# Stick-breaking q and k of a decoder trunk: products split as 512 + 256 columns, and products of 256 columns only

## What is computed

```python
u = rms_norm(h, mix_pre_g[i])
sb_q, sb_k, sb_v, df_q, df_k, df_v, g_sb, g_df = jnp.split(u @ w_in[i], split_at, axis=-1)

def stick_breaking_attention(q, k, v):          # 8 heads of 64
    z = einsum('bhqd,bhkd->bhqk', q_block, k) * 64 ** -0.5
    log_one_minus = where(strict, log_sigmoid(-z), 0.0)
    later = cumsum(log_one_minus, reverse) - log_one_minus
    w = where(strict, exp(log_sigmoid(z) + later), 0.0)
    return einsum('bhqk,bhkd->bhqd', w, v)
```

## Times and profile before

| | us |
|---|---|
| median of three runs | 1176.17 (1175.84 to 1176.51) |
| the profiled execution | 1175.95 |
| its span on the core | 1174.2 |
| busy: PE (matmul) | 1164.3 (99%) |
| busy: PEld (weight load) | 983.6 (84%) |
| busy: DVE (VectorE) | 849.9 (72%) |
| busy: ACT (ScalarE) | 720.6 (61%) |
| granted TensorE clock, share of full | 0.999 |

### The profile page before, as it was taken

How to read it: one execution, slowest core, us unless ns; L and a number is a source line. 1 busy time by engine, 2 the same in 40 slices (tenths; PEclk the granted TensorE clock), 3 DMA queues, 4 the chain that set the end, 5 groups by cost and what they waited for, 6 DMA issues and landing times.

```text
span 1174.2 us, 17191 instructions
## 1 busy us (share of the span) xinstructions
PE 1164.3 (99%) x6031; PEld 983.6 (84%) x6031; DVE 849.9 (72%) x1289; ACT 720.6 (61%) x1165; POOL 52.1 (4%) x122
## 2 busy tenths in 40 slices
PE   9999999999999999999999999999999999999997
PEld 7888888888888888888888888888888888888886
DVE  6766777877857776676787776678776677677666
ACT  7555556677755755555685655565776566565555
POOL 4000001000000000000100000010000010000002
PEclk9999999999999999999999999999999999999999
DMA  9656565554354565655556565746434456656550
GB/s 297 215 187 206 176 215 185 198 178 145 122 201 145 190 204 186 207 175 209 179 172 202 171 206 180 247 159 204 165 108 179 158 167 213 193 173 207 181 195 36
DMA packets 138655, 215.37 MB, mean 183 GB/s; under 512 B 6958, under 2 KB 97904, under 8 KB 138608
## 3 DMA queue, kind: packets, MB, share of 16 engines
q1 hardware_dynamic: 135808, 208.43, 53.1%
q10 hardware_dynamic: 2576, 6.29, 1.6%
q0 software_dynamic: 224, 0.04, 0.0%
HBM read 213.68 MB, written 1.05 MB: 183 GB/s over the span
## 4 chain that ended last, share of the span: by engine, by line
PE 99%; ACT 0%; DVE 0%; POOL 0%; issue 0%; DVEq 0%; POOLq 0%; ACTq 0%
PE ps L1626 23%; PE ps L1506 19%; PE ps L1508 18%; PE ps L1507 18%; PE ps L1636 12%; PE ps L1867 2%; PE ps L1553 2%; PE ps L1876 1%; PE ps L1753 1%; PE ps L1768 1%; PE ps L1727 0%; PE ps L1739 0%; PE ps L1782 0%; PE ps L1958 0%; PE ps L1789 0%; PE ps L1801 0%
## 5 line engine op out<-in xcount | busy, mean ns | idle before, releaser
L1077 DVE SCALAR_TENSOR_TENSOR w_lo<-raw,g_layer,w_hi 128x512 fp32r<-128x512 f32 (+1 forms) x504 | 356.4, 767 | 139.0 <-ACT w_hi L632 139.0
L632 ACT ACTIVATE w_hi<-raw,g_layer 128x512 fp32r<-128x512 f32 (+1 forms) x524 | 346.7, 732 | 113.7 <-PE ps L1636 97.0
L1626 PE MATMUL ps<-x_both,w_hi 128*128 128x512 f32 x1152 | 287.7, 392 | 0.0
L1626 PEld LDWEIGHTS ps<-x_both,w_hi 128*128 128x128 f32 x1152 | 209.4, 189 | 39.4 <-issue 0.4
L1506 PE MATMUL ps<-w_hi,x_both 128*128 128x512 f32 x576 | 231.1, 401 | 0.0
L1508 PE MATMUL ps<-w_hi,x_both 128*128 128x512 f32 x576 | 225.1, 391 | 0.0
L1507 PE MATMUL ps<-w_lo,x_both 128*128 128x512 f32 x576 | 224.6, 390 | 0.0
L1074 DVE TENSOR_TENSOR w_lo<-raw,w_hi 128x1024 fp32r<-128x1024 f32 x114 | 134.8, 1221 | 61.3 <-ACT w_hi L629 61.3
L629 ACT ACTIVATE w_hi<-raw 128x1024 fp32r<-128x1024 f32 x114 | 114.7, 1052 | 92.9 <-PE ps L1508 92.8
L1636 PEld LDWEIGHTS ps<-x_both,w_lo 128*128 128x128 f32 x1152 | 152.6, 191 | 8.4
L1636 PE MATMUL ps<-x_both,w_lo 128*128 128x256 f32 x1152 | 156.0, 283 | 0.0
(11 more groups left out here) (223 smaller groups left out, 1038.4 us busy)
## 6 DMA issues: line engine op xcount, KB each, us to landing
raw<-in_ffn_w_gu SPq DMA_DIRECT2D x170, 512.0 KB, 4.6
raw<-in_ffn_w_down SPq DMA_DIRECT2D x88, 512.0 KB, 4.0
raw<-in_w_in SPq DMA_DIRECT2D x80, 512.0 KB, 4.5
raw<-in_w_out SPq DMA_DIRECT2D x16, 512.0 KB, 4.0
raw<-in_w_ple_gate SPq DMA_DIRECT2D x16, 512.0 KB, 3.7
raw<-in_w_branch_sb SPq DMA_DIRECT2D x8, 512.0 KB, 4.2
raw<-in_w_branch_diff SPq DMA_DIRECT2D x8, 512.0 KB, 4.1
raw<-in_ffn_w_gu SPq DMA_DIRECT2D x12, 256.0 KB, 7.9
```

Source lines behind the costliest of these rows:

```text
L632: last = act.activation(w_hi[:, s, part], raw[:, s, part], ACT.Copy, scale=g_layer[:, g:g + 1])
L1077: last = dve.scalar_tensor_tensor(out=w_lo[:, s, part], in0=raw[:, s, part], scalar=g_layer[:, g:g + 1], in1=whi[:, part], op0=ALU.mult, o ...
L1626: mm = pe.matmul(dst, w_hi[:, s, cols], x_both[:, :, 4 * half + k, :], start=half == 0 and k == 0, stop=stop and k == 3, skip_group_check= ...
```

## The change

TensorE makes three products of 256 columns where it made one of 512 and one of 256. All three go to the left half of the bank, in the order `w_hi` by `x_hi`, `w_hi` by `x_lo`, `w_lo` by `x_hi` (`exact`, lines 1506 to 1508 before, 1487 to 1489 after). The right half of the banks is no longer used, ScalarE's copy and its scratch are gone, and VectorE reads the finished sum once from PSUM, multiplies by the constant and by the factors in one instruction, and writes q or k. It waits for TensorE's own signal of the finished product where it waited for ScalarE's copy. The waits on `flat_added` become waits on `sb_ready`.

```diff
@@ ScalarE
-            def keep_flat(i, j, x):
-                wait_product(act, win_done, 10 * i + j + 1, i, U_WIN + 2 * j + 1, x)
-                act.wait_ge(flat_added, 4 * i + 2 * (j - SBQ) + x)
-                act.activation(flat_copy, flat_pair(SB_FLAT[j][x])[1], ACT.Copy,
-                               scale=SB_D ** -0.5 if j == SBQ else 1.0).then_inc(flat_kept, 1)
...
-                    elif m in (5, 7):
-                        for x in range(2):
-                            high(i, U_WIN + m + 2, 8 + 4 * (m % 2), halves=(x,))
-                            keep_flat(i, m // 2, x)
@@ VectorE: def add_flat(i, j, x):
-                n = 4 * i + 2 * (j - SBQ) + x + 1
                 dst = (sbq_t, sbk_t)[j - SBQ][:, 2 * x:2 * x + 2, :]
-                dve.wait_ge(flat_kept, n)
-                dve.scalar_tensor_tensor(out=dst, in0=flat_pair(SB_FLAT[j][x])[0],
-                                         scalar=SB_D ** -0.5 if j == SBQ else 1.0, in1=flat_copy,
-                                         op0=ALU.mult, op1=ALU.add).then_inc(flat_added, 1)
-                dve.wait_ge(flat_added, n)
+                wait_product(dve, win_done, 10 * i + j + 1, i, U_WIN + 2 * j + 1, x)
                 dve.wait_ge(r_kept, nth_r(i, 1))
-                dve.tensor_tensor(dst, dst, r_cols.to_broadcast([P, 2, SEQ]), ALU.mult).then_inc(sb_ready, 1)
+                b = SB_FLAT[j][x]
+                dve.scalar_tensor_tensor(out=dst, in0=ps[:, b:b + 2, 0:SEQ], scalar=SB_D ** -0.5 if j == SBQ else 1.0,
+                                         in1=r_cols.to_broadcast([P, 2, SEQ]), op0=ALU.mult, op1=ALU.mult
+                                         ).then_inc(sb_ready, 1)
@@ TensorE: bank_free and flat_win
-                    pe.wait_ge(flat_added, 4 * i + 2 * (j - DFV) + 2)
+                    pe.wait_ge(sb_ready, 4 * i + 2 * (j - DFV) + 2)
...
-                        pe.wait_ge(flat_added, 4 * i + 1)
+                        pe.wait_ge(sb_ready, 4 * i + 1)
...
+                for n in range(2):
+                    for k in range(4):
+                        cols = slice(k * W + (2 * x + n) * P, k * W + (2 * x + n + 1) * P)
+                        mm = exact(bank(b + n)[:, 0:SEQ], w_hi[:, s, cols], w_lo[:, s, cols],
+                                   x_hi[:, 4 * half + k, :], x_lo[:, 4 * half + k, :],
+                                   half == 0 and k == 0, half == 1 and k == 3)
```

More of the change, by code:

```diff
@@ L182, in trunk_kernel @@
         df_slabs = [[x[:, t, 0:W] for t in range(TT)] for x in (tmp, gates[:, 0, :, :])]
-        flat_copy = w_att[:, :, 0:SEQ]
         minus = mixed_t[:, 0:P]
@@ L229, in trunk_kernel @@
         qk_turned = sem("qk_turned")
-        flat_kept = sem("flat_kept")
-        flat_added = sem("flat_added")
         sb_ready = sem("sb_ready")
@@ L325, in outs @@
             return bank(VALUE_BANK[n])[:, 0:SEQ].rearrange("p (t q) -> p t q", t=TT)
-        def flat_pair(b):
-            return [ps[:, b:b + 2, n * SEQ:(n + 1) * SEQ] for n in range(2)]
         def nth_r(i, stage):
@@ L1858, in flat_win @@
                     elif j == SBK:
-                        pe.wait_ge(flat_added, 4 * i + 1)
[L1861 to L1868, removed]
-                    return mm
[L1871 to L1884, removed]
+                        pe.wait_ge(sb_ready, 4 * i + 1)
[5 more added lines that the diff above has]
+                                   half == 0 and k == 0, half == 1 and k == 3)
+                if half == 0:
+                    return mm
                 if x == 0:
```

## The result

| | before | after |
|---|---|---|
| median, us | 1176.26 (1175.84 to 1176.77, 20 runs) | 1177.87 (1177.42 to 1178.36, 20 runs) |
| profiled execution, us | 1175.95 | 1177.97 |
| its span, us | 1174.2 | 1176.2 |

The ratio is 1.0013, 95% interval [1.0007, 1.0019]: slower by 1.6 us, clear of noise, and less than the 0.2% under which the prediction calls two times the same. 1177.6 us was forecast.

A forecast was written before the change was run, and what follows sets the result against it. PE (TensorE), busy 99% of the span, was taken as the bound. TensorE's 1.4 us plus 0 for VectorE and 0 for ScalarE, on a median of 1176.17, gave 1177.6 us, range 1176.3 to 1179.0.

The forecast's parts named there:

- The bound: Whole kernel and the changed stretches: PE busy 99% of the span and 25.00 of 25.00 us in each stretch.
- The term that decides: TensorE in stick-breaking q and k: 128 more products, 8 to 11 ns a pair, 1.0 to 1.4 us, taken as 1.4.
- The smaller extra that the prediction weighs: TensorE's added products by the Trainium skill's rule: 2.5 ns each, 0.3 us over 128 pairs, 1176.5 us.
- VectorE and ScalarE: Evacuations of q and k: VectorE relieved of 5.4 us, ScalarE of 4.8 us, 0 on the path.
- The waits that change hands: SBK's first product and the first scores, waiting for VectorE's evacuation: 1.0 and 1.2 us to spare, so no wait.
- if these covers were gone: Without spare time before PE needs q and k: at most one VectorE instruction per block, 2.8 us.
- A: TensorE's long runs of short products: weight loads set the pace at 141 ns, 9.5 us more, 1185.7 us; chance 0.05.
- B: Instruction fetch for added products and loads: one more packet not hidden costs 1.3 us, 1178.9 us; chance 0.05.
- C: PE's wait for ScalarE's copy of v: relief returns 0.7 of the 1.4 us, 1176.9 us; chance 0.06.

The follow-up runs named there:

- experiment 2: Changed kernel with TensorE's products as before (512 and 256 columns), keeping the new evacuation and omitting the high by low sum: 1176.05 us, ratio 0.9998.
- experiment 1: Kernel before, evacuation untouched, each long product of 512 columns in stick-breaking q and k given as two of 256: 1177.68 us, ratio 1.0012.
- experiment 5: Kernel before, each long product in stick-breaking q and k given as one of 384 and one of 128 columns: 1183.63 us, ratio 1.0063.
- experiments 6: Changed kernel with three more VectorE instructions ahead of each evacuation, into a scratch tile: 1181.58 us, ratio 1.0046.
- 7: Changed kernel with one more VectorE instruction ahead of each evacuation: 1177.82 us, ratio 1.0012.
- experiment 4: Kernel before, long products split into two of 256 columns in both feed-forward parts instead of q and k, 1152 products more: 1189.96 us, ratio 1.0115.
- Experiment 8: Changed kernel without the product of w_hi by x_lo, two products of 256 columns a pair: 1165.72 us, ratio 0.991.

## Why the prediction was right

**The bound.** PE 99% and full in the stretch: borne out. The evacuation alone gave 0 (experiment 2), and the products alone gave +1.3 us and the same stretch as the changed kernel (experiment 1).

**The term that decides.** 1.4 us was forecast for 128 more products. The two stretches grew by 0.72 and 0.70 us, 1.4 together. The medians are 1.6 us apart, which the uncertainty of 0.7 us on either side does not set apart from 1.4. Taking 120 ns and not 119 was right: the run of 96 shown above has 120. The prediction's reading of the earlier trace rows leaves one row out, though: 1.81 / 8 = 226 ns, where it says 228 to 230. With that row a pair before costs 345 ns, and the difference could have been up to 15 ns, 1.9 us, and not 11. The rows left that open, and the measured 0.72 us over 64 pairs, 11 ns each, closed it. The smaller extra that the prediction weighs, 2.5 ns a product or 0.3 us in all, lies outside the measured interval of 0.8 to 2.2 us.

**Why it holds was only half right.** The prediction read 13 to 15 ns beyond the columns as a fee that any product pays. At 256 and 512 columns that serves (120 and 227 to 230 ns, and 11.8 ns a product over 1152 of them). Below, it fails: in a run, a product of 128 columns takes 111 ns and not 67. That the reading held at 256 columns was a near thing, 120 ns against 111. The trace before held the warning. Its eight transposes, of 128 columns and with a load each, take 109 ns each (first line). Its stick-breaking part also has couples of one product of 384 and one of 128 columns, which take 0.29 us (the other lines), as in experiment 5:

```profile
227.44 0.87 PE ps L1727 x8
...
256.19 0.39 PE L1753 MATMUL ps<-sp_hi,neg_tri 128*128 128x384 f32 x1
256.42 0.22 PE L1754 MATMUL ps<-sp_hi,neg_one 128*128 128x128 f32 x1
256.48 0.39 PE L1753 MATMUL ps<-sp_lo,neg_tri 128*128 128x384 f32 x1
```

The prediction used neither. What the 13 to 15 ns beyond the columns are at 256 and 512 columns, no run here shows.

**VectorE and ScalarE.** The new instruction takes this long:

```profile
L1278 DVE SCALAR_TENSOR_TENSOR sbq_t<-ps,prob x4: 686/688/691, 232.7 to 815.9; 128x512 f32<-128x512 f32 x4
L1278 DVE SCALAR_TENSOR_TENSOR sbk_t<-ps,prob x4: 682/686/691, 245.1 to 828.3; 128x512 f32<-128x512 f32 x4
```

0.70 us was taken, 0.69 measured: reading with a spread factor costs it 4 ns at the most beside reading a whole tile (688 against 684 ns). VectorE was to come to 844.5 us and came to 845.0, ScalarE to 716 and came to 716.0.

**The waits that change hands.** The evacuations after:

```profile
232.68 0.69 DVE L1278 SCALAR_TENSOR_TENSOR sbq_t<-ps,prob 128x512 f32<-128x512 f32 x1
...
245.08 0.68 DVE L1278 SCALAR_TENSOR_TENSOR sbk_t<-ps,prob 128x512 f32<-128x512 f32 x1
```

q is out at 233.37 and SBK's first product starts at 234.64, so 1.27 us to spare where 1.0 was forecast; k is out at 245.76 and the scores start at 247.11, 1.35 us where 1.2 was forecast. The evacuation does not start at the same time as before, as the prediction had it: between the two profiles q's starts 0.7 us later and PE's arrival is 0.9 us later. That PE pays only for the part of a delay that exceeds this cover is shown by experiments 6 (2.2 us of delay, 3.7 us of time) and 7 (0.7 us, nothing). The price "if these covers were gone" was put at 2.8 us at the most, for one instruction a block. A longer delay costs more, as the 3.7 us show.

**The rivals.** A (loads become the pace in long runs of 256 columns) did not happen: 120 ns throughout, in the changed kernel's runs of 48 and 96 and in those of experiment 4. Its mechanism exists, but at 128 columns and at 111 ns, not at 256 and 141. The 141 ns came from dividing a row that holds the longer lead of the first load (0.22 us) and the last load's whole length (0.19). The kernel before has a row of sixteen such loads too:

```profile
63.48 2.09 PEld L1636 LDWEIGHTS ps<-x_both,w_lo 128*128 128x128 f32 x16
```

Sixteen take 2.09 us and eight 1.13, so eight more loads take 0.96 us, 120 ns each, the pace of their products. B: the instruction queue moved 29 packets after where it had 28. Two of them fall between 221 and 246 us, where it was one, and PE had no gap there, so the packet was hidden. C: PE still waits 0.7 us for the copy of v after the change.

No faster version that computes the same came out of this. The experiments point the other way, to as few products as possible, and of the forms tried here that compute all three parts the kernel before has the fewest. Experiment 8 is faster only because it leaves one part out.

## What to carry to other kernels

Where TensorE is full, count its products and not only its columns, and price them by the distance of their starts. Relief on an engine that TensorE does not wait for was worth nothing here, at 5 us and 4 us; but before TensorE is made faster, look which of those engines' signals it will then reach too early. Cutting a product cost a dozen nanoseconds where each piece took longer than the load of the next weights (256 and 256 columns), and some 57 ns where one did not (384 and 128).

## What was not expected of the hardware

- In a run, products of 128 columns, each with its own load of 128 x 128 weights, start 111 ns apart, not the 67 ns that the distances at 256 and 512 columns led to (120 and 227 to 230 ns).
- 384 beside 128 columns take 0.29 us a couple, in experiment 5 and in the kernel before. The small product is followed after 0.06 us, the large one only after 0.23, while the loads keep 0.11 and 0.18 us.
- At 256 columns it makes no difference whether the same weights come twice in a row (the changed kernel, experiment 1) or other ones each time (the short products of the earlier trace rows): 120 ns both ways. A load is recorded for every product all the same (6159 of each after the change).
